# Scaling and folding the odd modulation chunks on GpSimd, in a two-block transformer kernel

## The reference

```python
def second_block(x, c, ada_w, ada_b, norm1_w, ...):
    s = jax.nn.silu(c)
    for l in range(DEPTH):
        mod = s @ ada_w[l] + ada_b[l]        # 1024 values times a 1024 x 6144 matrix
        sh1, sc1, g1, sh2, sc2, g2 = [m[:, None, :] for m in jnp.split(mod, 6, axis=-1)]
        h = rmsnorm(x, norm1_w[l]) * (1.0 + sc1) + sh1
        ...
```

## Time and profile before

| | us |
|---|---|
| median of three runs | 3112.9 |
| profiled execution, its own time | 3126.6 |
| its span | 3124.8 |
| PE busy | 3001.6 (96%) |
| DVE busy | 1658.7 (53%) |
| ACT busy | 1390.7 (45%) |
| POOL busy | 418.2 (13%) |
| one chunk: ACT's scaling (8 instructions) | 3.30 |
| one chunk: DVE's two adds | 1.22 and 0.69 |

### The profile page before, as it was taken

One profiled execution on the slowest core, in us unless ns is written; L12 is line 12 of the kernel. 1 busy time (PEld: TensorE's weight loads), 2 busy tenths in 40 slices (PEclk: granted clock), 3 DMA queues, 4 the chain that ended last, 5 costly groups with the idle time before them and its releaser, 6 DMA issues.

```text
span 3124.8 us, 39078 instructions
## 1 busy us (share of the span) xinstructions
PE 3001.6 (96%) x16852; PEld 2721.6 (87%) x16852; DVE 1658.7 (53%) x1799; ACT 1390.7 (45%) x1601; POOL 418.2 (13%) x164
## 2 busy tenths in 40 slices
PE   7999998999999998999999999989999999999997
PEld 6888886998788887999799998889889989898896
DVE  2454212664355212565344443448777787777774
ACT  2554002443355101443223432247677677776774
POOL 1000000001000000000000000014333333343342
PEclk8999998999999999999899998989999999999998
DMA  9674622556476640455214555249999999999993
GB/s 294 208 234 158 208 81 69 187 176 185 162 234 204 194 136 27 162 200 165 97 62 168 175 177 162 63 141 374 340 347 357 344 365 336 347 360 334 359 346 150
DMA packets 392051, 678.86 MB, mean 217 GB/s; under 512 B 17184, under 2 KB 286528, under 8 KB 391744
## 3 DMA queue, kind: packets, MB, share of 16 engines
q1 hardware_dynamic: 389344, 666.82, 61.5%
q0 software_dynamic: 2528, 9.46, 1.0%
HBM read 675.19 MB, written 4.69 MB: 218 GB/s over the span
## 4 chain that ended last, share of the span: by engine, by line
PE 94%; DVE 3%; ACT 1%; issue 1%; DMA 0%; DVEq 0%; SPq 0%; POOL 0%
PE bank L498 93%; PE bank L1020 1%; PE bank L596 1%; DVE ka L1265 0%; DVE work L1126 0%; ACT w_hi L1671 0%; DVE probs L1165 0%; DVE peak L1149 0%; DMA const<-in_const 0%; ACT gates L1679 0%; DVE scores L1145 0%; DVE xT L1348 0%; ACT xT L1689 0%; DVE w_lo L1170 0%; DVE ew_lo L1577 0%
## 5 line engine op out<-in xcount | busy, mean ns | idle before, releaser
L1577 DVE TENSOR_TENSOR ew_lo<-ring_head,ew_hi 128x1792 fp32r<-128x1792 f32 (+1 forms) x288 | 680.7, 2397 | 199.5 <-ACT ew_hi L1888 199.5
L1888 ACT CAST ew_hi<-ring_head 128x1792 fp32r<-128x1792 f32 (+2 forms) x384 | 647.4, 1695 | 274.4 <-PE bank L498 274.4
L480 POOL TENSOR_TENSOR ew_lo<-ring_head,ew_hi 128x1792 fp32r<-128x1792 f32 (+1 forms) x96 | 389.3, 4055 | 1205.2 <-ACT ew_hi L1888 1205.2
L1170 DVE TENSOR_TENSOR w_lo<-ring_head,w_hi 128x2048 fp32r<-128x2048 f32 x108 | 247.5, 2292 | 224.8 <-ACT w_hi L1671 224.8
L1671 ACT CAST w_hi<-ring_head 128x2048 fp32r<-128x2048 f32 x108 | 205.2, 1903 | 300.9 <-PE bank L498 259.8
L498 PE MATMUL bank<-x_hi,w_hi 128*128 128x256 f32 x1152 | 323.9, 289 | 6.0 <-ACT x_hi L1689 6.0
L498 PE MATMUL bank<-x_hi,w_lo 128*128 128x256 f32 x1152 | 321.1, 286 | 0.0
L498 PE MATMUL bank<-x_lo,w_hi 128*128 128x256 f32 x1152 | 318.5, 283 | 0.0
L498 PE MATMUL bank<-ew_hi,xe_hi 128*128 128x448 f32 x1024 | 295.1, 370 | 4.4 <-DVE ew_lo L1577 4.4
L498 PE MATMUL bank<-ew_lo,xe_hi 128*128 128x448 f32 x1024 | 291.6, 366 | 0.0
L498 PE MATMUL bank<-ew_hi,xe_lo 128*128 128x448 f32 x1024 | 291.4, 366 | 0.0
(11 more groups left out here) (332 smaller groups left out, 4462.4 us busy)
## 6 DMA issues: line engine op xcount, KB each, us to landing
ring_head<-in_moe_w_gate SPq DMA_DIRECT2D x128, 896.0 KB, 6.6
ring_head<-in_moe_w_up SPq DMA_DIRECT2D x128, 896.0 KB, 6.8
ring_head<-in_moe_w_down SPq DMA_DIRECT2D x96, 1024.0 KB, 7.0
ring_head<-in_w_in SPq DMA_DIRECT2D x58, 1024.0 KB, 7.6
ring_head<-in_ffn_w_in SPq DMA_DIRECT2D x44, 1024.0 KB, 7.5
ring_head<-in_ada_w SPq DMA_DIRECT2D x30, 1024.0 KB, 5.4
ring_tail<-in_w_in SPq DMA_DIRECT2D x24, 1024.0 KB, 8.1
ring_head<-in_ffn_w_out SPq DMA_DIRECT2D x22, 1024.0 KB, 6.1
```

The source lines that it names most:

```text
L480: pool.tensor_tensor(ew_lo[:, h, 0:n], ring(c % 6)[:, 0:n], ew_hi[:, h, 0:n].bitcast(F32), ALU.subtract).then_inc(w_used[c % 6], 1)
L1170: v.tensor_tensor(w_lo[:, h, :], ring(s), w_hi[:, h, :].bitcast(F32), ALU.subtract).then_inc(w_used[s], 1)
L1577: v.tensor_tensor(ew_lo[:, h, 0:n], ring(c % 6)[:, 0:n], ew_hi[:, h, 0:n].bitcast(F32), ALU.subtract).then_inc(w_used[c % 6], 1)
L1888: a.copy(ew_hi[:, c % DEPTH_HI, 0:n], ring(c % 6)[:, 0:n]).then_inc(f.count(part_hi), 1)
```

## The change

Chunks with an odd number (12 of 24 in each layer) no longer go through ACT and DVE. GpSimd waits for the chunk's transfer, multiplies all 2048 elements by `cond` in one instruction, adds 1024 and then 512 elements, each once the one before has ended (semaphore `fold_step`), and counts `odd_ready`. PE waits for `odd_ready` before an odd chunk and for `mod_ready` before an even one. Even chunks are done as before. The order of PE's and SyncE's work is the same.

```diff
-    "inv_ready": 3, "lam_dot": 1, "lam_exp": 1, "mean_ready": 3, "merged_ready": 1, "mixer_in": 2, "mod_ready": 24,
-    "mod_scaled": 24, "par_in": 16, "peak_ready": 20, ...
+    "mod_ready": 12, "mod_scaled": 12, "odd_ready": 12, "par_in": 16, "peak_ready": 20, "probs_ready": 20,
...
@@ GpSimd, after the layer's bias transfers
+                    pool.wait_ge(cond_ready, 1)
+                    for c in range(24):
+                        s = ada_slot(c)
+                        w = tiles(ring(s), KD)
+                        f.bump(ada_loaded[s], 16)
+                        if c % 2 == 0:
+                            continue
+                        pool.wait_ge(ada_loaded[s], f.now(ada_loaded[s]))
+                        pool.tensor_tensor(w, w, cond[:, :].rearrange("p (k o) -> p k o", o=1).broadcast_to([P, KD, CW]), ALU.mult).then_inc(f.count(fold_step), 1)
+                        pool.wait_ge(fold_step, f.now(fold_step))
+                        pool.tensor_tensor(w[:, 0:4, :], w[:, 0:4, :], w[:, 4:8, :], ALU.add).then_inc(f.count(fold_step), 1)
+                        pool.wait_ge(fold_step, f.now(fold_step))
+                        pool.tensor_tensor(w[:, 0:2, :], w[:, 0:2, :], w[:, 2:4, :], ALU.add).then_inc(f.count(odd_ready), 1)
...
@@ PE, modulation(b, c)
-                pe.wait_ge(mod_ready, f.next(mod_ready))
+                folded = odd_ready if c % 2 else mod_ready
+                pe.wait_ge(folded, f.next(folded))
...
@@ DVE, the slot's folds
                         for c in fills(u):
 
+                            if c % 2:
+                                continue
                             w = tiles(ring(ada_slot(c)), KD)
...
@@ ACT, modulate(c)
                 s = ada_slot(c)
+                if c % 2:
+                    f.bump(ada_loaded[s], 16)
+                    return
                 w = tiles(ring(s), KD)
```

More of the change, by code:

```diff
@@ L100 @@
     "ffn_loaded1": 96, "ffn_loaded2": 96, "ffn_loaded3": 80, "ffn_loaded4": 80, "ffn_loaded5": 80, "ffn_summed": 4,
[1 row of a table removed]
-    "inv_ready": 3, "lam_dot": 1, "lam_exp": 1, "mean_ready": 3, "merged_ready": 1, "mixer_in": 2, "mod_ready": 24,
-    "mod_scaled": 24, "par_in": 16, "peak_ready": 20, "probs_ready": 20, "product_ready0": 6, "product_ready1": 5,
-    "rstd_ready": 3, "scalar_step": 2, "scaled": 12, "silu_ready0": 6, "silu_ready1": 5, "squares_ready": 12,
-    "std_ready": 3, "sub_squares": 1, "sub_std": 1, "summed": 4, "up_full0": 6, "up_full1": 5, "var_ready": 3,
[3 rows of a table removed]
-    "x_lo_ready": 4, "x_pieces": 6, "x_ready": 3,}
[1 row of a table added]
+    "hi_ready1": 16, "inv_ready": 3, "lam_dot": 1, "lam_exp": 1, "mean_ready": 3, "merged_ready": 1, "mixer_in": 2,
+    "mod_ready": 12, "mod_scaled": 12, "odd_ready": 12, "par_in": 16, "peak_ready": 20, "probs_ready": 20,
+    "product_ready0": 6, "product_ready1": 5, "rstd_ready": 3, "scalar_step": 2, "scaled": 12, "silu_ready0": 6,
+    "silu_ready1": 5, "squares_ready": 12, "std_ready": 3, "sub_squares": 1, "sub_std": 1, "summed": 4, "up_full0": 6,
[3 rows of a table added]
+    "w_used7": 9, "w_used8": 9, "x_hi_ready": 4, "x_lo_ready": 4, "x_pieces": 6, "x_ready": 3,}
 FFN1_TRIP = {
@@ L262, in program @@
         ada_loaded = [sem(f"ada_loaded{s}") for s in range(SLOTS)]
-        mod_scaled, mod_ready = sem("mod_scaled"), sem("mod_ready")
+        mod_scaled, mod_ready, odd_ready = sem("mod_scaled"), sem("mod_ready"), sem("odd_ready")
+        fold_step = sem("fold_step")
         ffn_loaded = [sem(f"ffn_loaded{s}") for s in range(6)]
```

## The result

The changed kernel takes 3185.5 us (median of 4 runs, 3182.4 to 3192.8) where the kernel before took 3115.5 on the same chip (4 runs, 3112.4 to 3119.1): a ratio of 1.0228, with an interval of 1.0204 to 1.0252. The forecast was 3182. The profiled execution has a span of 3190.9 us, 66.1 more than before (3124.8).

A forecast was written before the change was run, and what follows sets the result against it. TensorE, busy 96% of the span, bounds the kernel, so its new waits are paid in full. Waits 52.8 plus clock 20 less 4 for doubtful meetings give 69 us: 3196 profiled, 3182 for the runs, range 3136 to 3208.

The forecast's parts named there:

- The removed work at 0: Per layer, 40 us of ScalarE and 23 us of VectorE work removed beside a busy PE, counted as 0.
- The odd chunks in time, the semaphore free: GpSimd's 8.0 us per odd chunk fit within the 30 us between load and use; PE pays nothing.
- The port pair as the cost: GpSimd and VectorE exclude each other, delaying folds, normalise and rotary products up to 4.5 us; waits sum to 52.8 us.
- The multiply at 4.5 us: GpSimd's 2048-element multiply per odd chunk, taken as 4.5 us from two-input subtracts at 2.2 ns an element.
- The short waits: PE waits for even chunks' held second fold halves: 2.2 us each (15.4 in all) or 1.9 each (5.7).
- The meetings: Odd chunks land as VectorE folds, normalises or does the rotary step, in nearly every such slot: 17 waits, 52.8 us.
- The two doubtful ones: Meetings at chunk 10 of layer 0 and chunk 16 of layer 1, hanging on under 0.3 us; counted half, -4.
- The rotary step: In layer 0, GpSimd's work on chunk 1 delays L1210, for which PE waits, by 3.3 to 4.4 us; 4.4 taken.
- The clock at 20 us: Matmuls slowed at granted clock 0.50 behind PE's waits: 1.7 us for 12 of 17 waits, 20 us.
- Rival 1: VectorE keeps the pair between fold halves, so only multiplies begun earlier hold it up; 3138 us, chance 0.14.
- Rival 2: Not slower: GpSimd's work is hidden and VectorE's detours stay within the 2.26 us slack; 3113 us, chance 0.11.
- Rival 3: GpSimd's multiply is slower than the subtracts, 5.5 us, each of 17 holds 1 us longer; 3202 us, chance 0.13.

The follow-up runs named there:

- first experiment: The changed kernel with GpSimd only waiting for odd chunks and signalling, its three operations on them left out; ratio 1.0019 to the kernel before.
- the memsets: The changed kernel with three GpSimd memsets of 2048 elements in place of the multiply and two adds; ratio 0.9995 to the kernel before.
- the repeat: The unmodified changed kernel timed once more on another chip; 3188.0 us, ratio 1.0230 to the kernel before.
- the rotary step met alone: The changed kernel with GpSimd held until VectorE's fold in its way is done, except chunk 1, begun at landing; ratio 1.0000 to the kernel before.
- the longer multiply: The changed kernel with GpSimd multiplying the chunk by another full tile, memT, instead of the broadcast column; 3205.7 us, ratio 1.0290 to the kernel before.

## Why the prediction was right, and what was off

**The removed work at 0:** right (first experiment, 1.0019).

**The odd chunks in time, the semaphore free:** right; PE never waits for GpSimd.

**The port pair as the cost:** right as far as it says that the two engines exclude each other, and shown from both sides: with the meetings gone the cost is gone (1.0014), with late folds and no GpSimd work most of it is there (1.0179). That it hangs on GpSimd's reads is shown by the memsets, which held up no fold.

**The multiply at 4.5 us:** too long, it is 3.60. This is the mis-sized term. The nearest rows had two different stretches as inputs; with those the multiply does last 4.50 us. Each hold was 0.9 us shorter for it. The short waits fell by more, to 0.9 us where 2.2 was forecast: the second half is late by 3.3 us under a multiply of 3.60, so a hold is 0.3 less than the multiply, which the forecast took in full. Of the forecast's 52.8 us, 17 holds times 0.9 are 15, which leaves 37.5; measured are 39.2. That these two are so near is partly chance, since the groups moved in opposite directions: short ones 7.0 us (eight) for a forecast of 21.1 (ten), long ones 21.8 (seven) for 16.8 (four), chunk 20 twice 7.6 for 10.5, the rotary step 2.9 for 4.4.

**The meetings:** 17 were forecast, 18 found. Chunk 6 of layer 1 met, although I had read its landing as after the second half. Chunks 8 and 16 of layer 0 and 18 of layer 1 were forecast as short and were long (4.2, 2.7 and 2.7 us), because the multiply began before the first half, for the last two by 0.06 and 0.15 us. The two doubtful ones, counted half, both met. Chunks 2 and 12 of layer 0 and 12 of layer 1 stayed free, as forecast.

**The rotary step:** in this execution the multiply ended just before L1227, so only the two adds count. In the repeat it held L1227 for 1.1 us as forecast, and the wait grew by 4.0; with the rotary step met alone it grew by 4.5, against the forecast 4.4. L1233 was blocked, 1.76 us instead of 0.88. By the Trainium skill (SBUF — State Buffer, Who interferes with whom) a `tensor_scalar` from SBUF to SBUF can take both port pairs and is then blocked; the trace agrees with that.

**The clock at 20 us:** too small; it is 27, and about 34 with the longer multiply (half of 68.1 us more at 0.50). The price was wrong in both directions. The forecast took 1.7 us each for eight short and four long waits. Of the eight short ones only two had a stretch at 0.50 behind them, so they cost 3.4 us (half of 6.8) and not 13.6. The seven long ones had 41.0 us at 0.50, half of which is 20.5, or 2.9 each; and chunk 20, taken as 0, had 10.2 more, half of which is 5.1. The earlier trace rows already had 6.8 us at 0.50 behind a wait of 2.4, and the trace of before has 3.4 and 6.8 us behind equal waits of 3.36 for chunk 0 in its two layers: one price for every wait didn't follow from them.

So the mechanism was right, and two terms were mis-sized: 13.6 us of waits too many and 7 of clock too few. With the 4 us taken off for doubtful meetings they left 66.3 against the forecast 69. That the total is nearer than its parts is luck.

**Rival 1** (the pair stays with VectorE between the halves) fell: second halves of 3.98 us, and adds that get in between, at 286.40. **Rival 2** (hidden) fell: holds are 3.3 us against 2.26 of slack. **Rival 3** (a multiply slower than 4.5 us) had the direction wrong.

## What to carry to other kernels

Moving work to an idle GpSimd isn't free where VectorE's slack before TensorE is shorter than one GpSimd instruction: look at what VectorE does when GpSimd's data lands, since here a DMA released by the same event as the fold made them meet at 17 of the 20 folds of chunks 2 to 20. If they meet, start GpSimd behind VectorE's last due instruction, or cut its work into pieces shorter than the slack. And give an idle engine the work for which the busy one waits, not the work that is hidden: two chunks a layer brought 0.6%, twelve cost 2.3%.

## What the runs showed of the hardware that was not expected

- A GpSimd `tensor_tensor` of 2048 fp32 elements a partition took 3.60 us when its second input was a broadcast column or the very stretch of the first input, and 4.50 us when it was another tile; with the very stretch, multiply and subtract took the same. Why is open.
- A GpSimd memset didn't hold up VectorE's two-input folds (0.69 us in all 24), but did a `tensor_scalar` from SBUF to SBUF (1.28 us for two, 0.88 without).
- Of eight waits of 0.5 to 0.9 us in an otherwise busy stretch two were followed by 3.4 us at half the clock and six by none; in the repeat none of nine was. Waits of 2.7 us were followed by 3.4 or 6.8 us of it, without a visible reason for the one or the other. Over the mixers, waits of 39 us brought another 27 us of slower matmuls, and 11 us of waits removed gave 11 us back.
